# Hybrid attention, convolution and mixture-of-experts step: in each turn of the heads, the values of the head two back go ahead of the turn of the last head's probabilities

## What is computed

```python
q, k, v, ..., o_conv, q_na, k_na, v_na = mixer_inputs(x, shift1, scale1, lp)
# 8 latent-attention heads, 4 neighbourhood-attention heads; for each head:
s = q @ k.T * scale            # context rows see 128 keys, latent rows 384
p = softmax(s)
o = p @ v                      # 64 columns for each head
mix = concat(o_mla, o_conv, o_na)
x = x + gate1 * (mix @ w_out)
x = x + gate2 * grouped_moe(modulate(rms_norm(x)), ...)   # 16 experts, top 2 of one group
```

## Time and profile before

| | us |
|---|---|
| median of three runs | 1150.25 |
| the three runs | 1150.77, 1146.23, 1150.25 |
| the profiled execution, its own time | 1147.22 |
| its span in the profile | 1145.4 |
| TensorE busy | 1085.2 (95%) |
| VectorE busy | 881.7 (77%) |
| ScalarE busy | 701.5 (61%) |
| GpSimd busy | 228.2 (20%) |

### The profile page before, as it was taken

How to read it: one execution, slowest core, us unless ns; L and a number is a source line. 1 busy time by engine, 2 the same in 40 slices (tenths; PEclk the granted TensorE clock), 3 DMA queues, 4 the chain that set the end, 5 groups by cost and what they waited for, 6 DMA issues and landing times.

```text
span 1145.4 us, 14964 instructions
## 1 busy us (share of the span) xinstructions
PE 1085.2 (95%) x5668; PEld 864.1 (75%) x5668; DVE 881.7 (77%) x1077; ACT 701.5 (61%) x921; POOL 228.2 (20%) x213
## 2 busy tenths in 40 slices
PE   5899899999899999999999999889899999999996
PEld 2677556688778888888878877678878888888884
DVE  1368555674699999899975888865679999899894
ACT  2334265543487788888855357661278788887880
POOL 2201312011232221222101042211205121221100
PEclk9999899998999999999999998979899999999998
DMA  9866688845589999999952332113599999999971
GB/s 379 337 259 265 239 340 309 324 186 202 234 334 359 370 382 390 366 388 383 397 237 60 129 126 64 48 66 139 207 342 370 357 389 381 369 373 376 373 294 56
DMA packets 54298, 320.66 MB, mean 280 GB/s; under 512 B 11626, under 2 KB 11738, under 8 KB 19280
## 3 DMA queue, kind: packets, MB, share of 16 engines
q1 hardware_dynamic: 38448, 276.59, 62.6%
q0 software_dynamic: 15776, 43.08, 10.1%
HBM read 313.40 MB, written 25.44 MB: 296 GB/s over the span
## 4 chain that ended last, share of the span: by engine, by line
PE 75%; DVE 14%; DMA 3%; ACT 3%; issue 2%; POOL 1%; SPq 0%; DVEq 0%; POOLq 0%; ACTq 0%
PE bank L1272 40%; PE bank L901 6%; DVE w_lo L2427 5%; PE bank L1172 5%; PE bank L919 4%; PE bank L884 3%; DMA ring<-wring_dram 3%; PE bank L1031 3%; PE bank L962 2%; PE bank L996 2%; PE bank L1264 2%; PE bank L891 2%; PE bank L1208 1%; PE bank L929 1%; PE bank L1345 1%
## 5 line engine op out<-in xcount | busy, mean ns | idle before, releaser
L2427 DVE TENSOR_TENSOR w_lo<-ring,w_hi 128x2048 fp32r<-128x2048 f32 x192 | 436.4, 2288 | 42.7 <-ACT w_hi L1703 42.6
L1703 ACT CAST w_hi<-ring 128x2048 fp32r<-128x2048 f32 x192 | 367.2, 1917 | 35.2 <-PE bank L1272 34.8
L1272 PE MATMUL bank<-w_hi,hgT_hi 128*128 128x512 f32 x512 | 203.9, 398 | 6.5 <-issue 4.6
L1272 PE MATMUL bank<-w_hi,hgT_lo 128*128 128x512 f32 x512 | 200.9, 392 | 0.0
L1272 PE MATMUL bank<-w_lo,hgT_hi 128*128 128x512 f32 x512 | 200.8, 392 | 0.0
L812 POOL DMA_INDIRECT y_rows<-y,y_at x26 | 48.2, 1854 | 352.8 <-ACT y L1734 332.5
L1272 PEld LDWEIGHTS bank<-w_hi,hgT_hi 128*128 128x128 f32 x512 | 96.9, 189 | 27.4 <-issue 8.1
L1272 PEld LDWEIGHTS bank<-w_hi,hgT_lo 128*128 128x128 f32 x512 | 96.9, 189 | 20.5
L1272 PEld LDWEIGHTS bank<-w_lo,hgT_hi 128*128 128x128 f32 x512 | 97.1, 190 | 19.3
L1272 PE MATMUL bank<-w_hi,hidT_hi 128*128 128x512 f32 x256 | 102.3, 400 | 0.0
L1272 PE MATMUL bank<-w_hi,hidT_lo 128*128 128x512 f32 x256 | 100.2, 391 | 0.0
(11 more groups left out here) (303 smaller groups left out, 1817.8 us busy)
## 6 DMA issues: line engine op xcount, KB each, us to landing
ring<-wring_dram SPq DMA_DIRECT2D x258, 1024.0 KB, 8.2
y_rows<-hg POOLq DMA_DIRECT2D x6, 1024.0 KB, 6.2
kT<-mod_dram POOLq DMA_DIRECT2D x4, 1024.0 KB, 8.6
late<-y_rows POOLq DMA_DIRECT2D x4, 1024.0 KB, 14.6
ring<-wring_dram SPq DMA_DIRECT2D x4, 832.0 KB, 10.4
h_rows<-h_tok POOLq DMA_DIRECT2D x6, 512.0 KB, 2.9
ring<-wring_dram SPq DMA_DIRECT2D x4, 640.0 KB, 10.7
bias<-na_bias_dram POOLq DMA_DIRECT2D x32, 64.0 KB, 6.6
```

What stands on the lines that cost most here:

```text
L1272: mm = pe.matmul(b[:, :], a, w[m], start=(start and k == 0), stop=(stop and k == 2))
L1703: act.copy(w_hi[:, q, :], in_ring(l, expert_slot(e, i))).then_inc(hi_made[q], 1)
L2427: dve.tensor_tensor(w_lo[:, q, :], in_ring(l, expert_slot(e, i)), w_hi[:, q, :], ALU.subtract) \
```

## The change

Within a turn, `values(i - 2)` now stands between `scores(i)` and `turn_probs(i - 1)`, on TensorE and in the list that deals out the banks. No instruction is added or removed; ScalarE, VectorE, GpSimd and the DMA queues keep their order. The bank numbers that they read change with the list.

```diff
@@ psum_plan
         if i == 0:
             order += [("q", 1, t) for t in range(3)] + [("kv", 1, t) for t in range(4)]
+
+        if i >= 2:
+            order += [("O", i - 2)]
         if 1 <= i <= len(GROUPS):
             order += [("PT", i - 1, 0), ("PT", i - 1, 1)]
-        if i >= 2:
-            order += [("O", i - 2)]
         if i == len(GROUPS):
@@ TensorE's loop over the turns
                     if i == 0:
                         queries(l, 1)
                         keys_values(l, 1)
+                    if i >= 2:
+                        values(l, i - 2)
                     if 1 <= i <= len(GROUPS):
                         turn_probs(l, i - 1)
-                    if i >= 2:
-                        values(l, i - 2)
                     if i == len(GROUPS):
```

## The result

The changed kernel took 1162.87 us in the median (four executions, 1159.91 to 1166.03), against 1149.6 for the kernel before (four, 1146.23 to 1150.77). The ratio is 1.0115, with a 95% interval of 1.0081 to 1.0148: 1.2% slower. The profiled execution took 1162.72 us, its span is 1160.9. The prediction was 1151.65, in a range up to 1156.0, with a chance of 0.14 for slower. One thing is needed to read what follows: single executions of one kernel here differ by 10 us or more, by whether a long stretch at half clock comes in layer 1, so I give the median and the spread over all executions beside the ratio.

What follows compares the result with a forecast made beforehand. The chain was taken as mostly TensorE, largely the experts' products, with delays in the heads reaching the end. Terms -1.25 + 2.05 + 0.6 = +1.4 us on the median of 1150.25 gave 1151.65, range 1146.0 to 1156.0.

Steps and rivals of the forecast that it cites:

- Layer 1, turns 7 to 9: Later bank wait and values waiting for a copy in turn 9: +0.9 us at VectorE's statistics, bounds 0 and 1.2.
- The sum for layer 1: All of layer 1's heads, with half clock taken in turns 10 to 12: +0.6 us.
- The third rival: Regular turns of layer 1 at half clock, 7.84 us each: four add about 15 us, to 1167; chance 0.02.
- Turn 10 of layer 1: TensorE's gap shrinks from 3.09 to about 2.2 us, ahead of three transposes, and half clock follows.
- The 0.8 us wait of turn 9: Layer 1: values of head 7 wait for a copy ending at 740.26, no longer covered by transposes; 0.6 us more.
- the longer idle of turn 2: Layer 1: values of head 0 wait for the copy until 696.75, so TensorE idles 0.8 to 0.9 us longer.
- Layer 0, turn 12: Values of head 10 wait for a copy, later transposes delay ScalarE's silu: +2.05 us, bounds 0.7 and 2.1.
- no slack: Layer 0, turn 12: ScalarE's 2.05 us delay at the silu was taken to reach the end in full.
- The slower rival for this place: Layer 0, turn 12: a new fall of the clock adds 4.5 us, giving 1156.2; chance 0.13.
- Layer 0, turns 2 to 7: VectorE waits less for values of heads 0 and 4: -1.25 us, bounds -1.3 and 0.
- a forecast of +0.8: All of layer 0: -1.25 us from turns 2 to 7 and +2.05 us from turn 12.
- The main rival on the slow side: A new clock fall in layer 0, turn 12, +5.9 us in all, to 1156.2; chance 0.13.

Runs made afterwards that it cites:

- kernel 3: Values first in every turn but turn 7 of layer 1, against the kernel before: 1153.12 us, ratio 1.0.
- kernel 4: The kernel before with values first in turn 7 of layer 1 alone: 1161.86 us against 1149.99, ratio 1.0081.
- kernel 7: The kernel before with only the list of banks in the new order, in turn 7 of layer 1: 1158.26 us against 1151.01, ratio 1.0055.
- kernel 8: The kernel before with only TensorE's order changed, in turn 7 of layer 1, banks as before: 1149.83 us against 1151.01, ratio 0.9985.
- kernel 1: Values first in layer 0 alone, layer 1 in the order of before: 1152.72 us against 1149.78 for the kernel before, ratio 1.0006.
- kernel 6: The full change, with VectorE's outputs of head 5 ahead of its mask addition in turn 7 of layer 1: 1152.51 us against 1149.99 for before.
- kernel 11: The kernel before, layer 1: head 5's outputs ahead of the mask addition in turn 7, 13 identity products in turn 10's gap: 1144.87 us against 1151.01.
- kernel 2: Values first in layer 1 alone, against the kernel before: 1158.67 us, ratio 1.0047.

## Why the prediction was wrong, point by point

**The step that failed is "Layer 1, turns 7 to 9".** The prediction saw the mechanism: the bank for which TensorE waits falls two places earlier, and nine transposes follow that wait in place of three. It priced it as transposes alone, +0.3, and never asked what the longer gap does to the clock, a question it did ask in turn 10. The gap grew from 0.76 to 1.62 us, the same size as the one of turn 2 that it took as proof that short gaps suffice. It lies behind another gap of 1.12 us. The clock fell there in the profiled execution and stayed down for 37 us, and kernels 3, 4, 7 and 8 show that this turn, and in it the dealing of banks, is worth 7 to 12 of the 13 us. That 727 to 733 had kept its clock with 57% busy was read as safe; it was near an edge, for in kernels 1 and 3, with the old banks in this turn, the clock did fall there.

**The sum for layer 1, +0.6, was short by about 8.** Layer 1 alone measured +8.9. The third rival, regular turns at half clock, described what happened: a turn of 7.95 us, forecast 7.84. It had a chance of 0.02, since I looked for its trigger in the small waits of the regular turns. Here the Trainium skill (TensorE: Matmul & The Clock Gate, section "A second HAM failure mode: psum-queue depth-cycling"), which says that cycling through PSUM banks can make the clock swing, pointed the right way. Its mechanism, small idle spells between the groups, is not what this trace has: one wait for a bank stands ahead of the stretch, there is no gap over 0.1 us within it, and the clock does not swing but stays down. The price was below 15 us. Turns 8 to 11 were hit, four as in the rival, but from the values of turn 10 on the kernel before was at half clock too: some 13.6 us of its time between 730 and 790, against 37.5 now. The difference of 24 us at half clock is worth some 12 us of work (an estimate), of which the lost gap of 3.09 us gives a part back; the table has 8.6.

**Turn 10 of layer 1 was right** where it could be seen: 2.2 us forecast ahead of three transposes, 2.17 measured in kernel 3, and a fall of the clock behind it. In the full change the clock was already low. The 0.8 us wait of turn 9 (0.81) came as worked out, and so, nearly, did the longer idle of turn 2 (2.40, not 1.67; forecast 0.8 to 0.9 more).

**Layer 0, turn 12: +2.05 forecast, +2.4 measured** in the table (from +4.7 to +7.1), with a wait of 2.33 us on ScalarE. That it would all reach the end ("no slack") can't be seen here: the falls of the clock between 275 and 320 us differ by more than that between the two profiles. The clock did not fall in turn 12; it fell briefly from 242 on, behind a wait of 0.48 us at the output product. The slower rival for this place, a fall between 228 and 240, did not come.

**Layer 0, turns 2 to 7: -1.25 forecast, -0.55 measured** (+1.95 to +1.4). VectorE's wait for head 0 went to nothing, that for head 4 from 1.31 to 0.54, which is 0.77, the lead of the values. The prediction took the 0.5 us gained at head 0 off the same wait. That was an error in the sum: what head 0 gains moves TensorE's scores and VectorE alike. The output of head 4 did come 1.1 us earlier (0.9 us later on the clock, less the 1.95 from before the heads), but half of it was lost again, and the first turned queries came 0.3 us earlier and not 1.2. For turn 7 had the same bank trouble as in layer 1, small:

```profile
192.39 0.36 DVE L1984 TENSOR_TENSOR xn<-bank,rowsum 128x192 f32<-128x192 f32 x1 [0.54 <-PE bank L997]
```
```profile
201.37 1.50 PE L885 MATMUL bank<-shapes,qk 128*64 128x128 f32 x12 [0.52 <-DVE xn L1984]
```

Behind it the clock fell from about 208 to 214 (scores of turn 9 are 4.6 us late, those of turn 8 only 1.4), which is more than the whole gain. Such a fall between 205 and 215 stands in six of the seven profiles with the new order in this turn, and in none of the seven with the old one. It was absent in kernel 1's profiled execution, which took 1153.41 all the same. Kernel 1 measured +2.9 for all of layer 0 by the medians, against a forecast of +0.8, and how much of that the fall makes stays open.

**The range** was built on bounds of the waits, and left the clock's worst case in turn 7 out. The main rival on the slow side stood at the wrong turn.

## What to carry to other kernels

Moving an entry in a list that deals out PSUM banks changes who waits for whom far behind the moved work; follow each bank to its next user, above all where groups of many banks (here the turned heads) meet a reader that is busy with something else. Price every gap that grows on TensorE twice, once as idle time and once as a possible stretch at half clock, and weigh neighbouring gaps together. Where such a gap can't be shortened, products that nobody reads can fill it, and where the reader's own order makes it, moving that reader's instruction ahead can take it away; here that cost nothing that could be seen (kernels 6 and 11).

## What was not expected of the hardware

A fall of the granted clock outlasted its cause by far. After the gaps of turn 7 the changed kernel's TensorE has no gap over 0.1 us from 739 to 774, and yet its clock stays at 1.2 GHz for some 37 us (735 to 775: 0.53, busy 38.4 of 40). In turn 2 it came back after some 7 us in the kernel before and 3.4 in the changed one. In turns 2 to 4 TensorE does mostly transposes and 96-row scores, in turns 8 to 11 scores with 64 rows; whether that matters was not tried, and it is not all of it, for in kernel 2 the clock came back within the 64-row scores of turn 10, after 20 us, where it stayed down in the full change. So what ends such a stretch stays open. The same gaps do not always have the same effect: with two gaps of 1.12 and about 0.4 us, kernel 8 lost the clock in the profiled execution, and eight of its ten executions took under 1151 us. So what the change did was mainly to turn a rare event (16 of 97 executions of the kernel before are at or above 1157 us, with the low mean clock) into one that came in each of the 4 of the full change, and in each of the 10 of kernels 2 and 4. What length the stretch had in those that were not profiled is not known; one of the four (1159.91) has a mean clock of 0.968 and not 0.960.
